# Second norm of a layer: from scaled rows to a product with a diagonal, with the rows for the experts made by GpSimd

## The reference, cut to what matters

```python
def rmsnorm(x, g):
    return x * rsqrt(mean(x * x, axis=-1, keepdims=True) + EPS) * g

for l in range(2):
    h = rmsnorm(x, norm1_g[l])
    ...                                   # y_a, y_b, y_c from h @ w_in[l]
    x = x + concatenate([y_a, y_b, y_c]) @ w_out[l]
    h2 = rmsnorm(x, norm2_g[l])           # <- the second norm
    x = x + hier_moe(h2, rg_w[l], rg_b[l], re_w[l], re_b[l], w_gate[l], w_up[l], w_down[l])
return rmsnorm(x, final_g)

def hier_moe(t, ...):
    g_prob = softmax(t @ rg_w + rg_b)     # router, 4 groups: takes all rows of h2
    e_logits = t @ re_w + re_b            # router, 4 experts in each group
    # the best group, the two best experts in it, their gates
    # each expert: (silu(t @ w_gate) * (t @ w_up) * gate) @ w_down, on its own tokens
```

## Time and profile before

| | us |
|---|---|
| runs, median (lowest to highest) | 1243.47 (1241.18 to 1243.91) |
| the profiled execution | 1238.99 |
| its span | 1237.2 |
| PE busy | 1149.7 (93%) |
| DVE busy | 1009.5 (82%) |
| ACT busy | 739.3 (60%) |
| POOL busy | 121.8 (10%) |
| mean busy share of the DMA engines in 304 to 306 us | 0.24 |

### The profile page before, as it was taken

One profiled execution on the slowest core, in us unless ns is written; L12 is line 12 of the kernel. 1 busy time (PEld: TensorE's weight loads), 2 busy tenths in 40 slices (PEclk: granted clock), 3 DMA queues, 4 the chain that ended last, 5 costly groups with the idle time before them and its releaser, 6 DMA issues. The chain is left out here.

```text
span 1237.2 us, 17552 instructions
## 1 busy us (share of the span) xinstructions
PE 1149.7 (93%) x5752; PEld 910.3 (74%) x5752; DVE 1009.5 (82%) x1607; ACT 739.3 (60%) x1054; POOL 121.8 (10%) x157
## 2 busy tenths in 40 slices
PE   5999978998999999999799999789989999999985
PEld 4876855787788888888678577458787888888874
DVE  5898986347699999999579899762668999999994
ACT  5234248432688888888442332682427888888882
POOL 4100000001011111010400000000000111011141
PEclk9999989999999999999899999799999999999997
DMA  9722211218899999999844122003389999999985
GB/s 299 280 93 83 85 35 34 69 35 318 274 391 394 392 393 392 393 392 380 169 160 132 55 86 68 35 19 102 119 287 324 392 394 391 393 392 393 390 238 147
DMA packets 145819, 291.36 MB, mean 236 GB/s; under 512 B 17120, under 2 KB 19216, under 8 KB 145728
## 3 DMA queue, kind: packets, MB, share of 16 engines
q1 hardware_dynamic: 130176, 237.63, 53.7%
q0 software_dynamic: 15552, 52.59, 13.2%
HBM read 264.46 MB, written 25.69 MB: 235 GB/s over the span
## 5 line engine op out<-in xcount | busy, mean ns | idle before, releaser
L372 PE MATMUL ps<-w_hi,a_hi 128*128 128x512 f32 x960 | 381.3, 397 | 17.3 <-DVE a_lo L1441 11.6
L360 ACT ACTIVATE w_hi<-raw 128x1024 fp32r<-128x1024 f32 (+1 forms) x256 | 268.1, 1054 | 206.1 <-PE ps L374 199.5
L374 PE MATMUL ps<-w_hi,a_lo 128*128 128x512 f32 x960 | 375.4, 391 | 0.0
L373 PE MATMUL ps<-w_lo,a_hi 128*128 128x512 f32 x960 | 375.2, 391 | 0.0
L364 DVE TENSOR_TENSOR w_lo<-raw,w_hi 128x1024 fp32r<-128x1024 f32 (+1 forms) x256 | 302.6, 1210 | 75.1 <-ACT w_hi L360 67.2
L364 DVE TENSOR_TENSOR w_lo<-arena,w_hi 128x1024 fp32r<-128x1024 f32 x192 | 227.5, 1221 | 8.6 <-ACT w_hi L360 0.4
L360 ACT ACTIVATE w_hi<-arena 128x1024 fp32r<-128x1024 f32 x192 | 203.8, 1063 | 43.1 <-PE ps L374 38.4
L372 PEld LDWEIGHTS ps<-w_hi,a_hi 128*128 128x128 f32 x960 | 181.1, 189 | 55.5 <-issue 16.6
L374 PEld LDWEIGHTS ps<-w_hi,a_lo 128*128 128x128 f32 x960 | 181.0, 189 | 38.4
L373 PEld LDWEIGHTS ps<-w_lo,a_hi 128*128 128x128 f32 x960 | 181.3, 189 | 35.7
L372 PE MATMUL ps<-a_hi,w_hi 128*128 128x512 f32 (+1 forms) x304 | 122.7, 404 | 5.6 <-DVE a_lo L1256 5.6
(11 more groups left out here) (237 smaller groups left out, 1229.8 us busy)
## 6 DMA issues: line engine op xcount, KB each, us to landing
arena<-in_w_down SPq DMA_DIRECT2D x144, 256.0 KB
raw<-in_w_gate SPq DMA_DIRECT2D x136, 256.0 KB, 2.7
raw<-in_w_up SPq DMA_DIRECT2D x136, 256.0 KB, 3.0
arena<-in_w_gate SPq DMA_DIRECT2D x120, 256.0 KB
arena<-in_w_up SPq DMA_DIRECT2D x120, 256.0 KB
raw<-in_w_down SPq DMA_DIRECT2D x112, 256.0 KB, 9.5
raw<-in_w_in SPq DMA_DIRECT2D x80, 256.0 KB, 6.9
y_rows<-arena POOLq DMA_DIRECT2D x42, 256.0 KB, 5.9
```

Source lines behind the costliest of these rows:

```text
L360: nc.scalar.activation(split_slot(w_hi, n, w), place(S, i, n, w), ACT.Copy).then_inc(S.w_hi_set, 1)
L372: nc.tensor.matmul(o, lh, rh, start=start, stop=False)
L373: nc.tensor.matmul(o, lh, rl, start=False, stop=False)
L374: return nc.tensor.matmul(o, ll, rh, start=False, stop=stop)
```

## The change

In the second norm alone (k odd):

- DVE doesn't write the row. It writes a 128x128 tile `diag2[tt]` = identity * (1/rms), and `hrow_set` now counts these.
- PE doesn't transpose `hrow`. It multiplies: `x` (the raw tile, stationary) with `diag2[tt]` (moving), a float32 matmul of 128x128 for each of the 32 pieces. Its result is the transposed and scaled `x`, still without the weight vector.
- The weight vector is now a column for each channel (`gcol2`, loaded once): ACT's copy to `a_hi` takes it as its scale, and DVE's `a_lo` is (bank * column) - `a_hi` in one instruction.
- POOL makes the rows that the experts gather: for each tile a product with 1/rms, then a product with `gain`, each 128x1024, both in `hrow`. It stores all four tiles after the last of them is made. Between its two products of a tile it waits for the first.
- Two semaphores of the attention part are made one (`inadm_set` goes into `idx_acc`, with other counts). This changes no order.

```diff
@@ gpsimd
+            pool.dma_start(gcol2[:], t["norm2_cols"]).then_inc(tiny_in, 16)
...
                 for tt in range(TT):
-                    pool.wait_ge(hrow_set, 4 * k + tt + 1)
+                    pool.wait_ge(hrow_set, TT * k + tt + 1)
+                    if tt == 0:
+                        pool.wait_ge(gain_in, 16 * (k + 1))
+                    g.tensor_scalar(hrow[:, tt, :], x[:, tt, :], nrm[:, 3, tt:tt + 1], None, ALU.mult).then_inc(h2_rows, 1)
+                    pool.wait_ge(h2_rows, 2 * TT * l + 2 * tt + 1)
+                    g.tensor_tensor(hrow[:, tt, :], hrow[:, tt, :], gain[:], ALU.mult).then_inc(h2_rows, 1)
+                for tt in range(TT):
+                    pool.wait_ge(h2_rows, 2 * TT * l + 2 * tt + 2)
                     pool.dma_start(h2d[l][tt * P:(tt + 1) * P, :], hrow[:, tt, :]).then_inc(h2_stored, 16)
@@ tensor, norm_transposes
-                        mm = T.transpose(ps[:, c, tt * P:(tt + 1) * P], hrow[:, tt, c * P:(c + 1) * P], ident)
+                        o = ps[:, c, tt * P:(tt + 1) * P]
+                        if k % 2:
+                            mm = T.matmul(o, x[:, tt, c * P:(c + 1) * P], diag2[:, tt, :], start=True, stop=True)
+                        else:
+                            mm = T.transpose(o, hrow[:, tt, c * P:(c + 1) * P], ident)
@@ scalar, norm_hi
+                    if k % 2:
+                        g = DC * (k // 2) + c
+                        A.activation(a_hi[:, c, :], ps[:, c, :], ACT.Copy, scale=gcol2[:, g:g + 1]).then_inc(ht_hi, 1)
@@ vector, norm_rows
-                        if w == 0:
-                            ve.wait_ge(gain_in, 16 * (k + 1))
-                        V.scalar_tensor_tensor(out=hrow[:, w, :], in0=x[:, w, :], scalar=nrm[:, 3, w:w + 1], in1=gain[:],
-                                               op0=ALU.mult, op1=ALU.mult).then_inc(hrow_set, 1)
+                        if k % 2:
+                            V.tensor_scalar(diag2[:, w, :], ident, nrm[:, 3, w:w + 1], None, ALU.mult).then_inc(hrow_set, 1)
+                        else:
+                            row_scale(k, w)
@@ vector, norm_lo
+                    if k % 2:
+                        g = DC * (k // 2) + c
+                        V.scalar_tensor_tensor(out=a_lo[:, c, :], in0=ps[:, c, :], scalar=gcol2[:, g:g + 1],
+                                               in1=a_hi[:, c, :].bitcast(F32), op0=ALU.mult, op1=ALU.subtract).then_inc(ht_lo, 1)
@@ vector, attention scores
-                    V.memset(mask[b][0:CHUNK, KEYS[b] - CHUNK:KEYS[b]], NEG_INADM).then_inc(inadm_set, 1)
-                ve.wait_ge(inadm_set, 3 * (l + 1))
+                    V.memset(mask[b][0:CHUNK, KEYS[b] - CHUNK:KEYS[b]], NEG_INADM).then_inc(idx_acc, 1)
+                ve.wait_ge(idx_acc, 27 * (l + 1))
```

More of the change, by code:

```diff
@@ L149, in trunk @@
         gslot = sb("gslot", [P, TILES])
+        gcol2 = sb("gcol2", [P, DEPTH * DC])
         ovx = sb("ovx", [P, EXTRA + 1], I32)
@@ L192, in trunk @@
         lgT = ar(A_P, SEQ)
+        diag2 = ar(A_P, TT * P, TT, P)
         slot_hot = ar(A_P, TT * TOPE * P, TT * TOPE, P)
@@ L241, in trunk @@
             sem(n) for n in ("qi_set", "ki_set", "u_set", "sig_set", "glu_set", "k_set", "q_set", "v_set"))
-        wt_ready, widx_set, dots_ready, relu_set, idx_acc, inadm_set, topk_step = (
-            sem(n) for n in ("wt_ready", "widx_set", "dots_ready", "relu_set", "idx_acc", "inadm_set", "topk_step"))
+        wt_ready, widx_set, dots_ready, relu_set, idx_acc, topk_step = (
+            sem(n) for n in ("wt_ready", "widx_set", "dots_ready", "relu_set", "idx_acc", "topk_step"))
         conv_tap, pool_d, pw_in = sem("conv_tap"), sem("pool_d"), sem("pw_in")
@@ L257, in trunk @@
                              "tab_ready", "tab_set", "ovx_set"))
-        h2_stored = sem("h2_stored")
+        h2_rows, h2_stored = sem("h2_rows"), sem("h2_stored")
         yc_in = [sem(f"yc_in{q}") for q in range(TT * TOPE)]
@@ L595, in norm_transposes @@
                         spin(0, 2)
-                    pe.wait_ge(hrow_set, 4 * k + tt + 1)
+                    pe.wait_ge(hrow_set, TT * k + tt + 1)
                     for c in range(DC):
@@ L873, in other @@
                             pe.wait_ge(pool_d, l + 1)
[L874 removed]
+                            pe.wait_ge(tiny_in, 16 * (3 + 4 * DEPTH))
                         else:
@@ L975, in norm_hi @@
                     sc.wait_ge(ht_ready, DC * k + c + 1)
-                    A.activation(a_hi[:, c, :], ps[:, c, :], ACT.Copy).then_inc(ht_hi, 1)
+                    if k % 2:
+                        g = DC * (k // 2) + c
+                        A.activation(a_hi[:, c, :], ps[:, c, :], ACT.Copy, scale=gcol2[:, g:g + 1]).then_inc(ht_hi, 1)
+                    else:
+                        A.activation(a_hi[:, c, :], ps[:, c, :], ACT.Copy).then_inc(ht_hi, 1)
             def tile_xt(S, i, c):
@@ L1210, in norm_rows, with row_scale @@
                         link(V.reciprocal(nrm[:, 3, w:w + 1], nrm[:, 2, w:w + 1]))
-                        if w == 0:
-                            ve.wait_ge(gain_in, 16 * (k + 1))
-                        V.scalar_tensor_tensor(out=hrow[:, w, :], in0=x[:, w, :], scalar=nrm[:, 3, w:w + 1], in1=gain[:],
-                                               op0=ALU.mult, op1=ALU.mult).then_inc(hrow_set, 1)
+                        if k % 2:
+                            V.tensor_scalar(diag2[:, w, :], ident, nrm[:, 3, w:w + 1], None, ALU.mult).then_inc(hrow_set, 1)
+                        else:
+                            row_scale(k, w)
+            def row_scale(k, w):
+                if w == 0:
+                    ve.wait_ge(gain_in, 16 * (k + 1))
+                V.scalar_tensor_tensor(out=hrow[:, w, :], in0=x[:, w, :], scalar=nrm[:, 3, w:w + 1], in1=gain[:],
+                                       op0=ALU.mult, op1=ALU.mult).then_inc(hrow_set, 1)
             def add_mixed(l, tt):
@@ L1255, in norm_lo @@
                     ve.wait_ge(ht_hi, DC * k + c + 1)
-                    V.tensor_tensor(a_lo[:, c, :], ps[:, c, :], a_hi[:, c, :].bitcast(F32), ALU.subtract).then_inc(ht_lo, 1)
+                    if k % 2:
+                        g = DC * (k // 2) + c
+                        V.scalar_tensor_tensor(out=a_lo[:, c, :], in0=ps[:, c, :], scalar=gcol2[:, g:g + 1],
+                                               in1=a_hi[:, c, :].bitcast(F32), op0=ALU.mult, op1=ALU.subtract).then_inc(ht_lo, 1)
+                    else:
+                        V.tensor_tensor(a_lo[:, c, :], ps[:, c, :], a_hi[:, c, :].bitcast(F32), ALU.subtract).then_inc(ht_lo, 1)
             def topk_round(l, r):
@@ L1472, in _ @@
                 if l == 0:
-                    ve.wait_ge(tiny_in, 16 * (2 + 4 * DEPTH))
+                    ve.wait_ge(tiny_in, 16 * (3 + 4 * DEPTH))
                     link(V.tensor_copy(rw_hi[:], rw[:]))
@@ L1688 @@
         t[name] = t[name].rearrange("l g e a b -> (l g e) a b")
+    cols = np.ascontiguousarray(np.asarray(inputs["norm2_g"]).reshape(DEPTH, DC, P).transpose(2, 0, 1).reshape(P, DEPTH * DC))
+    arrays["in_norm2_cols"] = cols
+    t["norm2_cols"] = nc.dram_tensor("in_norm2_cols", cols.shape, mybir.dt.from_np(cols.dtype), kind="ExternalInput").ap()
     out = nc.dram_tensor("out_0", (1, SEQ, D), F32, kind="ExternalOutput").ap()
```

6 lines of the change are left out of this document (3 added, 3 removed).

## The result

| | before | changed |
|---|---|---|
| median, same chip (lowest to highest), us | 1242.65 (1241.18 to 1243.91) | 1260.6 (1258.29 to 1266.74) |
| executions | 5 | 5 |
| ratio | | 1.0151, 95% interval 1.0128 to 1.0175 |
| the profiled execution / its span, us | 1238.99 / 1237.2 | 1266.74 / 1264.9 |
| POOL busy, us | 121.8 | 166.9 |

The change costs 18 us, about six times the 2.9 that were forecast, and the time lies outside the range. The profiled execution of before is 3.7 us under its median and that of the changed kernel 6.1 over it, so the traces differ by 27.7. I read stretches from them, and sizes from the ratios and medians. One disturbed execution, of 2311.79 us in experiment 2, is left out of the comparisons.

The account below looks back on a forecast made before the run. PE was taken to bound the second norm, with DVE also near the limit. PE's products 0.9, evictions 0.13 and gather 0.4 give 1.43 us per layer, 2.9 over two: 1243.47 + 2.9 = 1246.4 us, range 1243.2 to 1253.

Parts of the forecast that it names:

- PE's products: Second norm: float32 products replace transposes, 16 records and 1.81 us for a tile, +0.9 us in each layer.
- DVE's saving: Second norm: diagonals replace rows, DVE gains 2.9 us in each layer, none counted because it only turns into waiting.
- The evictions: Second norm: scaled a_hi and a_lo copies take longer; only the first of each is on the path, +0.13 us per layer.
- POOL's rows: GpSimd's two products take 0.97 and 1.94 us, 3.5 a tile with waits; work ends at 290.3, rows stored about 297.
- (b): Rival: POOL products of 2.7 us or more make rows late, delaying gather and PE; 1256 us at 3.3 us; chance 0.08.
- the term for the gather: First expert's gather: weight loads held behind the stores run into it, PE loses up to 0.8, 0.4 us per layer taken.
- (a): Rival: DVE and POOL block each other, diagonal of tile 1 +1.0, before route +0.5 in each layer; 1249.4 us; chance 0.32.

Follow-up runs that it names:

- experiment 2: As experiment 1, but GpSimd still makes its eight products, into a free buffer behind the stores, with nobody waiting for them: 1255.68 us, ratio 1.0107.
- Experiment 3: As experiment 1, without products, but the four stores of raw x wait until the route is set: 1253.46 us, ratio 1.0088.
- experiment 10: Kernel before with ten filler products at the very start, ahead of PE's first transposes: 1242.17 us against 1243.12, ratio 0.9985.
- experiment 7: Changed kernel with 22 more filler products in each layer in PE's wait for the route: 1256.27 us, ratio 1.0112.
- experiment 1: Changed kernel without GpSimd's eight products; raw x is stored as soon as the diagonal is there: 1249.68 us against 1242.33, ratio 1.0062.
- experiment 8: Changed kernel with rows made by DVE, no fillers between the second norm's tiles, and 20 fillers in the wait for the route: 1246.10 us, ratio 1.0037.
- 11: Changed kernel with rows made by DVE and the two fillers between the second norm's tiles left out: 1243.45 us against 1243.12, ratio 1.0001.
- 9: Changed kernel with the experts' rows made by DVE and only stored by GpSimd, fillers unchanged: 1248.15 us against 1243.12, ratio 1.0025.
- experiment 4: Changed kernel with GpSimd's second product of each tile also a product with a scalar, weight vector left out of the rows: 1256.97 us, ratio 1.0117.
- experiment 12: Changed kernel with rows by DVE, no fillers between the second norm's tiles, and ten fillers at the very start: 1245.94 us against 1242.82, ratio 1.0028.
- 5: Kernel before with ten more filler products in each layer in PE's wait for the route: 1241.96 us, ratio 1.0000.
- experiment 6: Kernel of experiment 1 with ten more filler products in each layer in PE's wait for the route: 1247.46 us, ratio 1.0045.

## Why the prediction was wrong

**PE's products: right.** 16 records for each tile and no idle time between the tiles. The tiles are 2.23 us apart, 2.28 were worked out. Measured from the start of the norm, the last router product comes 0.8 later, where 0.9 and the 0.13 of the evictions were worked out. DVE's saving bought nothing, as said.

**The evictions: right.** `a_lo` lasts 5.36 us for 8, 0.67 for each, as forecast; `a_hi` doesn't delay it.

**POOL's rows: this step failed.** The term gave 3.5 us for a tile and the last store issued at 292.7; measured are 5.3 us and 301.3, and the rows had landed at about 306 instead of 297. It took 0.97 us from a memset for the product with the scalar and doubled it for the other, 2.9 for a tile, and said itself that no row gives an upper bound. Measured: 2.85 and 2.34. The order is the reverse of the one assumed: the instruction with one large input is the slower. The Trainium skill (GPSIMD Engine Reference, Elementwise — side-by-side cycle accounting), which had been weighed at 2.25 us as an estimate, is close to the 2.34 to 2.38 of the trace (the page's own figure is for an addition). The Trainium skill (GPSIMD Engine Reference, Engine selection) calls one input "roughly line-rate" on GpSimd; 2.85 us for 1024 elements, where DVE's row took 1.28, speaks against it. The memset was the nearest row and the wrong neighbour: it reads nothing.

**Two rivals at once.** (b) was to decide from 2.7 us in the mean on, and the mean is 2.7, but the waits between the products are shorter than it took: the last product ends at 299.1, not past 300.5, and the rows have landed at about 306, not past 307.2. The gather doesn't wait for the rows themselves, as the table is later still; what costs is the other half of the rival, the loads that were held behind `h2_stored` and now stand in the gather's way. PE waits 3.33 us for it in layer 0, where the term for the gather had 0.4 in each layer. Experiment 3 prices the late rows at 3.8 us for both layers. The rival had a chance of 0.08, since its own condition was measured against a guess. (a) was right in its mechanism and too small: it foresaw +1.0 for the diagonal of tile 1, which ran free in 0.29, and +0.5 ahead of the route. The diagonal that was held, the last, didn't matter (PE wanted it at 284). That a slower POOL would reach the route's small instructions it said, but gave it no price; it took 2.35 us of layer 0. Experiment 2 prices it at 6.0 us for both layers against the 3.0 of the rival. The chances treated the two as alternatives, though one cause, a slow GpSimd, drives both; with the measured prices the sum is 1246.4 - 0.8 + 3.8 + 6.0 = 1255.4, outside the range too and still 5 short.

**PE's clock stood nowhere in the sum.** PE idle for 5.6 us is followed by 10.2 us at half clock, and the fillers behind it, which PE must run through before the table's products, last 5.68 instead of 4.40. But they last 5.89 in layer 0 of experiment 10, behind 2.43 us of idle time and with the work of before, so this number alone doesn't tell what the longer wait costs. Filling the wait goes with 4 us less in the changed kernel (experiment 7: ratio 1.0112 against 1.0151, intervals that overlap a little), 2 less in that of experiment 1 and none in that of before; and experiment 8, which has the fillers, has a higher ratio than 11, which doesn't (1.0037 against 1.0001). A price for the clock is therefore not shown.

**What isn't settled.** Experiments 1 and 9 leave 7.4 and 3 to 5 us for PE's form of the norm, where the prediction has 2.1. If differences of 0.3% aren't evidence, up to 4 us of this can be any edit's. Why 1 is slower than 9, though it does less, was not tried; they also ran on different chips. The prices of 2 and 3 are taken from 1, and so they hang on it. What is shown is that 11 to 15 of the 18 us go when GpSimd makes no products, and that with the products the trace shows DVE held, late rows and a late gather.

## What to carry to other kernels

Work that goes to GpSimd beside a busy DVE must be priced twice, by its own duration and by the DVE instructions beside it, those with two SBUF inputs above all, each of which may last as long as GpSimd's; and where the trace has no row for it, the range must take in the case that it is three times slower than the nearest row. Rivals that hang on the same unknown number belong into one case, and their prices add up. Before a difference of 0.3% is explained, an edit that does nothing should be timed as well.

## What the hardware showed that was not expected

- GpSimd's TENSOR_SCALAR on 128x1024 float32 (2.85 us, the scalar read from SBUF for each partition) is slower than its TENSOR_TENSOR (2.34 to 2.38).
- A DVE instruction of 0.17 us lasts 2.12 beside GpSimd's TENSOR_TENSOR, and a split of 1.22 us runs free beside its TENSOR_SCALAR (experiment 4). In a chain of small instructions one is caught and the others pass before and behind it.
- The same 2.43 us of PE idle time in layer 0 were followed by half clock until 300.6 in one trace (before), until about 304 in two others (experiments 1 and 10), and by none in that of experiment 12.
- PE stands still for up to 4.3 us in the sum of the experts' outputs, with no wait shown, in six of the fourteen traces (0.8 us or more: experiments 3, 5, 6, 7, 8 and 10). In experiment 6 the DMA engines are full with the gathers of these outputs when it begins, at 612.6 (share 1.03 and 1.08). ACT has such a pause in every trace, also in that of before:

```profile
613.88 1.28 ACT L961 ACT_TABLE_LOAD   x1 [4.21 <-issue]
```

The Trainium skill (Runtime: NRT & Kernel Launch, Instruction fetch mechanics) has each engine's instructions fetched by DMA in blocks of 16 KiB. In the pause of experiment 6 the profile has a packet of 16 KB of a queue that it calls instruction (q8), between 614 and 615 us. That such a fetch waits behind the gathers would fit, but is only argued.
